# A hybrid encoder layer in fp32: a key product moved to GpSimd, small steps moved to VectorE, ScalarE's order changed in the bidirectional HGRN2 scan

## The reference

```python
f = lb_dir + (1.0 - lb_dir) * jax.nn.sigmoid(f_logits)
kh = 1.0 - f ;  lfh = log(f)
b = jnp.cumsum(log_f, axis=3)                  # in chunks of 32 tokens
scores = (q * exp(b - b_mid)) @ (k * exp(b_mid - b))
contrib = (k * exp(b_last - b)).T @ v ;  decay = exp(b_last)
S_t = decay * S_{t-1} + contrib ;  o = tril(scores) @ v + (q * exp(b)) @ S_{t-1}
o = rmsnorm(o_forward + o_backward, norm_g) * silu(g)
```

## Time and profile before

| what | value |
|---|---|
| median of three runs | 1166.91 us (1166.90 to 1168.83) |
| the profiled execution: own time, span | 1168.83 us, 1166.9 us |
| TensorE busy | 1152.8 us (99%) |
| VectorE, ScalarE, GpSimd busy | 632.5, 457.6, 107.3 us (54%, 39%, 9%) |
| the HGRN2 stage | about 582 to 705 us of the span |

### The profile page before, as it was taken

The page is one execution under the profiler, slowest core; times in us unless marked ns, Lnnn a source line. Parts: engine busy times, 40 slices in busy tenths (PEclk is TensorE's granted clock), DMA queues, the critical chain, the costliest instruction groups (busy, mean ns, idle before and its releaser), DMA issues.

```text
span 1166.9 us, 15661 instructions
## 1 busy us (share of the span) xinstructions
PE 1152.8 (99%) x5879; PEld 935.7 (80%) x5879; DVE 632.5 (54%) x760; ACT 457.6 (39%) x674; POOL 107.3 (9%) x88
## 2 busy tenths in 40 slices
PE   9999999999999999999999999999999999999997
PEld 7888888888888777777778788888888888888886
DVE  6755555543333674444488976656455555552223
ACT  6423322322223444544757745534332232231223
POOL 0000000000001220000057620011000000000000
PEclk9999999999999999999999999999999999999999
DMA  5332233242224232112131122432232322323221
GB/s 202 110 108 101 78 108 107 84 145 97 87 91 168 87 116 72 55 56 71 37 109 38 37 74 91 162 102 97 90 109 90 108 90 90 108 90 108 90 90 72
DMA packets 31677, 111.63 MB, mean 96 GB/s; under 512 B 3984, under 2 KB 5136, under 8 KB 31376
## 3 DMA queue, kind: packets, MB, share of 16 engines
q1 hardware_dynamic: 30192, 104.11, 26.6%
q10 hardware_dynamic: 1440, 6.88, 1.6%
HBM read 105.48 MB, written 4.19 MB: 94 GB/s over the span
## 4 chain that ended last, share of the span: by engine, by line
PE 94%; DVE 2%; ACT 1%; DMA 1%; issue 1%; POOL 0%; ACTq 0%; DVEq 0%; SPq 0%; POOLq 0%
PE ps L1154 25%; PE ps L1156 25%; PE ps L1155 25%; PE ps L1189 3%; PE ps L1188 3%; PE ps L1190 3%; PE ps L1294 1%; PE ps L1303 1%; PE ps L1319 1%; DMA raw<-up_dram 1%; PE ps L1438 1%; PE ps L1421 1%; PE ps L1446 1%; PE ps L1402 0%; DVE w_lo L763 0%
## 5 line engine op out<-in xcount | busy, mean ns | idle before, releaser
L1154 PE MATMUL ps<-h_hi,w_hi 128*128 128x512 f32 x1024 | 408.0, 398 | 0.2 <-DVE w_lo L763 0.2
L1156 PE MATMUL ps<-h_hi,w_lo 128*128 128x512 f32 x1024 | 399.3, 390 | 0.0
L1155 PE MATMUL ps<-h_lo,w_hi 128*128 128x512 f32 x1024 | 399.1, 390 | 0.0
L763 DVE TENSOR_TENSOR w_lo<-raw,w_hi 128x1024 fp32r<-128x1024 f32 (+2 forms) x190 | 233.2, 1230 | 192.5 <-ACT w_hi L419 186.1
L419 ACT ACTIVATE w_hi<-raw 128x1024 fp32r<-128x1024 f32 (+1 forms) x182 | 196.0, 1080 | 172.7 <-PE ps L1156 96.1
L1154 PEld LDWEIGHTS ps<-h_hi,w_hi 128*128 128x128 f32 x1024 | 192.4, 188 | 56.5 <-issue 16.7
L1155 PEld LDWEIGHTS ps<-h_lo,w_hi 128*128 128x128 f32 x1024 | 192.6, 188 | 41.6 <-issue 2.9
L1156 PEld LDWEIGHTS ps<-h_hi,w_lo 128*128 128x128 f32 x1024 | 192.3, 188 | 40.7
L489 ACT ACTIVATE g_hi<-un 128x512 f32 (+1 forms) x44 | 27.8, 632 | 250.8 <-DVE un L763 250.8
L763 DVE TENSOR_TENSOR un<-ps,rs 128x512 f32<-128x512 f32 x44 | 30.4, 691 | 122.2 <-PE ps L1156 122.2
L1154 PE MATMUL ps<-g_hi,w_hi 128*128 128x512 f32 x176 | 68.5, 389 | 0.0
(11 more groups left out here) (238 smaller groups left out, 1239.6 us busy)
## 6 DMA issues: line engine op xcount, KB each, us to landing
raw<-up_dram SPq DMA_DIRECT2D x86, 512.0 KB, 3.2
raw<-proj_dram SPq DMA_DIRECT2D x26, 512.0 KB, 3.3
raw<-down_dram SPq DMA_DIRECT2D x16, 704.0 KB, 4.0
raw<-down_dram SPq DMA_DIRECT2D x22, 512.0 KB, 3.2
raw<-gates_dram SPq DMA_DIRECT2D x16, 512.0 KB, 3.2
raw<-branch_dram SPq DMA_DIRECT2D x8, 512.0 KB, 3.2
raw<-wout_dram SPq DMA_DIRECT2D x8, 512.0 KB, 3.2
x_spill_dram<-xT ACTq DMA_DIRECT2D x1, 2048.0 KB, 7.3
```

The source lines that it names most:

```text
L763: return V.tensor_tensor(out, a, b, op)
L1154: T.matmul(ps[:, bank, :], w_hi[:, slot, cols], moving_hi(j), start=start and j == 0, stop=False)
L1155: T.matmul(ps[:, bank, :], w_hi[:, slot, cols], moving_lo(j), start=False, stop=False)
L1156: ins = T.matmul(ps[:, bank, :], w_lo[:, slot, cols], moving_hi(j), start=False, stop=stop and j == tiles - 1)
```

## The change

- `k_in` is no longer made by ScalarE but by GpSimd, in a new function `key`: a `tensor_scalar` of 128x512 with a scale and a bias for each partition. ScalarE's logarithm, which overwrites its input, waits for it. Keys 0 and 1 are made ahead of GpSimd's loop, key u+2 between `key_to_end` and `values`.
- The 128x16 `fac` difference goes from GpSimd's `to_end` to the end of VectorE's `cumulate`.
- The product with the output gate goes from GpSimd (`gate_outputs`) to VectorE's `normalize`; so does the gain, which had been folded into `silu`. `norm_exp` loses its square, and `normalize` has five operations in place of three.
- Within `exponentials`, `decay` is made ahead of `k_sc` and `k_end`.
- In ScalarE's loop `outputs_to_sbuf` goes behind `exponentials(u + 2)`.
- `WARM` goes from 11 to 8.

```diff
-        FIRST_UNITS, PARTS, PART, WARM, WARM_BANK = 2, 4, UW // 4, 11, 7
+        FIRST_UNITS, PARTS, PART, WARM, WARM_BANK = 2, 4, UW // 4, 8, 7
@@ GpSimd
+            def key(u):
+                pool.wait_ge(fs_done, u + 1)
+                if u == 0:
+                    pool.wait_ge(s_done, 2 * ITEMS)
+                if u >= 2:
+                    pool.wait_ge(ks_done, u - 1)
+                nc.gpsimd.tensor_scalar(k_in[u % 2][:], forget[:, u, :], lb_minus_one[:, u:u + 1], one_minus_lb[:, u:u + 1],
+                                        ALU.mult, ALU.add).then_inc(k_done, 1)
             def to_end(u):
                 pool.wait_ge(b_done, u + 1)
-                if u >= 2:
-                    pool.wait_ge(kfar_done, u - 1)
-                nc.gpsimd.tensor_tensor(fac[:, u % 2, :, :], upper, lower, ALU.subtract).then_inc(fd_done, 1)
-            def gate_outputs(t):
-                nc.gpsimd.tensor_tensor(o_t[:], o_t[:], hgate[:, t, :], ALU.mult).then_inc(og_done, 1)
                 key_to_end(u + 1)
-                if u and u % 2 == 0:
-                    gate_outputs(u // 2 - 1)
+                if u + 2 < TILES:
+                    key(u + 2)
                 if u % 2:
                     values(u // 2 + 1)
@@ ScalarE
             def log_f(u):
-                A(k_in[u % 2][:], forget[:, u, :], ACT.Identity, bias=one_minus_lb[:, u:u + 1],
-                  scale=lb_minus_one[:, u:u + 1]).then_inc(k_done, 1)
+                act.wait_ge(k_done, u + 1)
                 A(forget[:, u, :], forget[:, u, :], ACT.Ln, bias=lb[:, u:u + 1], scale=one_minus_lb[:, u:u + 1]).then_inc(lf_done, 1)
             def exponentials(u):
                 A(fac[:, u % 2, :, :], fac[:, u % 2, :, :], ACT.Exp).then_inc(fac_done, 1)
+                A(decay[u % 2].rearrange("p (e n) -> p e n", n=NSUP)[:, :, n],
+                  ends.unsqueeze(1).to_broadcast([P, HD, NSUP - 1]), ACT.Exp).then_inc(e5_done, 1)
                 A(k_sc[u % 2][:], k_sc[u % 2][:], ACT.Exp, scale=-1.0).then_inc(e2_done, 1)
                 A(k_end[:], k_end[:], ACT.Exp).then_inc(e3_done, 1)
-                A(decay[u % 2].rearrange("p (e n) -> p e n", n=NSUP)[:, :, n],
-                  ends.unsqueeze(1).to_broadcast([P, HD, NSUP - 1]), ACT.Exp).then_inc(e5_done, 1)
             def norm_exp(t):
-                A(o_u[:], o_rs[:], ACT.Square).then_inc(oy_done, 1)
@@ ScalarE's loop
-                if u % 2:
-                    outputs_to_sbuf(u // 2)
                 if u + 2 < TILES:
                     exponentials(u + 2)
                 if u and u % 2 == 0:
                     yb_hi(u // 2 - 1)
+                if u % 2:
+                    outputs_to_sbuf(u // 2)
@@ VectorE, cumulate
+                if u % 2:
+                    tt(fac[:, 1, :, :], b6[:, :, 16:33:16], b6[:, :, 32:49:16], ALU.subtract).then_inc(fd_done, 1)
+                else:
+                    tt(fac[:, 0, :, :], b6[:, :, 31:48:16], b6[:, :, 15:32:16], ALU.subtract).then_inc(fd_done, 1)
             def normalize(t):
-                link(stt(o_u[:], o_u[:], -0.5, o_ms[:], ALU.mult, ALU.mult))
-                link(stt(o_rs[:], o_u[:], 1.5, o_rs[:], ALU.add, ALU.mult))
-                tt(o_u[:], o_t[:], o_rs[:], ALU.mult).then_inc(on_done, 1)
+                link(newton(o_rs[:], o_ms[:], o_u[:]))
+                link(stt(o_t[:], o_t[:], gain[:, 34 + t:35 + t], o_rs[:], ALU.mult, ALU.mult))
+                tt(o_u[:], o_t[:], hgate[:, t, :], ALU.mult).then_inc(on_done, 1)
```

More of the change, by code:

```diff
@@ L318, in _ @@
             supers = lambda t: t.rearrange("p (n c) -> p n c", c=SUPER)
+            def key(u):
[6 more added lines that the diff above has]
+                                        ALU.mult, ALU.add).then_inc(k_done, 1)
             def to_end(u):
                 pool.wait_ge(b_done, u + 1)
-                b3 = supers(b_cum[u % 2][:])
-                if u >= 2:
-                    pool.wait_ge(kfar_done, u - 1)
-                upper, lower = (b3[:, :, 16:33:16], b3[:, :, 32:49:16]) if u % 2 else (b3[:, :, 31:48:16], b3[:, :, 15:32:16])
-                nc.gpsimd.tensor_tensor(fac[:, u % 2, :, :], upper, lower, ALU.subtract).then_inc(fd_done, 1)
                 if u == 0:
@@ L331, in to_end @@
                     pool.wait_ge(kt_done, u)
+                b3 = supers(b_cum[u % 2][:])
                 end = b3[:, :, 0 if u % 2 else SUPER - 1]
@@ L364, in values @@
                                             ALU.mult).then_inc(vexp_done, 1)
-            def gate_outputs(t):
-                pool.wait_ge(osq_done, t + 1)
-                pool.wait_ge(sil_done, HH)
-                nc.gpsimd.tensor_tensor(o_t[:], o_t[:], hgate[:, t, :], ALU.mult).then_inc(og_done, 1)
             pool.wait_ge(spilled, 16)
             nc.gpsimd.memset(q_pad[1], 0.0).then_inc(pad_zeroed, 1)
+            key(0)
+            key(1)
             pool.wait_ge(sil_done, HH)
@@ L389, in _ @@
                     to_end(u + 2)
-            gate_outputs(PAIRS - 1)
             pool.wait_ge(mean_done, 2)
@@ L641, in exponentials @@
                 A(q_sc[:], k_sc[u % 2][:], ACT.Exp).then_inc(e1_done, 1)
+                if u >= 2:
+                    act.wait_ge(state_done, u - 1)
                 act.wait_ge(fd_done, u + 1)
                 A(fac[:, u % 2, :, :], fac[:, u % 2, :, :], ACT.Exp).then_inc(fac_done, 1)
+                n = slice(first, first + NSUP - 1)
+                ends = b[:].rearrange("p (n c) -> p n c", c=SUPER)[:, n, end]
+                A(decay[u % 2].rearrange("p (e n) -> p e n", n=NSUP)[:, :, n],
+                  ends.unsqueeze(1).to_broadcast([P, HD, NSUP - 1]), ACT.Exp).then_inc(e5_done, 1)
                 act.wait_ge(e1_done, u + 1)
@@ L948, in silu @@
                 dve.wait_ge(sl_done, j + 1)
[L949 to L953, removed]
+                dst = (hq, hgate)[j // 4][:, j % 4, :]
+                tt(dst, dst, silu_tmp[j % 4][:], ALU.mult).then_inc(sil_done, 1)
             base = BASE["proj"]
@@ L1016, in cumulate @@
                 tt(chunks(k_sc[u % 2][:]), b3, mid.unsqueeze(2).to_broadcast([P, 2 * NSUP, CHUNK]), ALU.subtract).then_inc(d1_done, 1)
[L1018 to L1024 removed]
+                b6 = supers(b[:])
+                if u % 2:
+                    tt(fac[:, 1, :, :], b6[:, :, 16:33:16], b6[:, :, 32:49:16], ALU.subtract).then_inc(fd_done, 1)
+                else:
+                    tt(fac[:, 0, :, :], b6[:, :, 31:48:16], b6[:, :, 15:32:16], ALU.subtract).then_inc(fd_done, 1)
+            def normalize(t):
+                dve.wait_ge(or_done, t + 1)
+                link(newton(o_rs[:], o_ms[:], o_u[:]))
+                link(stt(o_t[:], o_t[:], gain[:, 34 + t:35 + t], o_rs[:], ALU.mult, ALU.mult))
+                tt(o_u[:], o_t[:], hgate[:, t, :], ALU.mult).then_inc(on_done, 1)
                 dve.wait_ge(on_done, t + 1)
```

10 lines of the change are left out of this document (removed).

## The result

The changed kernel takes **1175.02 us** (median of 4 runs, 1174.26 to 1175.46) against 1166.91, a difference of the medians of +8.1 us. The ratio by all runs is 1.0065, interval 1.0052 to 1.0078. The forecast was 1169.5. The direction was right, the size was off by 5.5 us.

A forecast was written before the change was run, and what follows sets the result against it. TensorE, busy 1152.8 of 1166.9 us, was taken as the bound. 2.2 later at pair 1's `mean_square`, less 1.3, plus a 1.7 clock fall gave +2.6: profiled 1171.4, median 1169.5; own range 1168 to 1171.5, overall 1163.6 to 1172.6.

The forecast's parts named there:

- So 2.0 are left: VectorE's path to the scan of tile 3: 2.0 us of lead left, scan ending at 644.8 in place of 646.8.
- I take nothing: Start: three fewer warm products lengthen TensorE's idle time to about 1.4 us, at no cost; bounds nothing and 1.7.
- Then the same difference holds: Step from profiled time to median: +2.6 applies even if the other runs had no clock fall at A.
- A: TensorE's wait at HGRN2 entry (line 1421, until 601.85): all 1.6 us goes, and the 1.7 clock fall behind it.
- B: TensorE's wait at line 1391 for tile 3, about 1.2 us, ended by ScalarE's mean copy: goes.
- D: TensorE's wait at line 1391 for tile 5 (657.69), 1.28 us, ended by ScalarE's mean copy: goes.
- C: TensorE's wait at line 1438 (646.94), 1.2 us, for VectorE's state scan of tile 3, forecast to end 2.0 earlier.
- The exchange without a fall: Rival 1: waits move as forecast but the clock stays: +0.9, 1167.8 us; chance 0.27.
- The second (all waits go): Rival 2: waits go and none replaces them, scan ending by 641.6; 1160.0 us, halfway 1163.4; chance 0.20.
- The third (keys crowd VectorE): Rival 3: keys 2 to 5 beside VectorE's products delay the scan 3.9 us: 1173.4, at half 1171.5; chance 0.13.
- The fourth, the warm-up: Rival 4: the shorter warm-up costs up to +1.7 us; chance counted within the others.
- D's 1.3 come back: Sum at `mean_square` of pair 1: 2.2 us later, less 1.3 regained from wait D, gives +0.9.

The follow-up runs named there:

- key_decay_order: Kernel before with three queue edits: keys on GpSimd, `decay` ahead, `outputs_to_sbuf` behind the exponentials; `fac`, `normalize`, warm-up as before: 1169.51 us.
- plus_fac: key_decay_order with the `fac` difference also on VectorE: 1171.77 us.
- fac_alone: Changed kernel with one added wait in GpSimd's `to_end`, so `fac` on VectorE never runs beside `k_end`: 1172.83 us.
- plus_norm: key_decay_order with the new `normalize` (gate product, gain and square on VectorE) added: 1171.86 us.
- before_warm8: Kernel before with `WARM` 8 in place of 11, nothing else: 1167.79 us.
- order_only: Kernel before with only ScalarE's order changed, exponentials ahead of `outputs_to_sbuf`: 1170.35 us.
- the best version: keys01_order1: kernel before with keys 0 and 1 on GpSimd and the new ScalarE order in tile 1 alone: 1165.55 us.
- mean_first: Kernel before with ScalarE's copy of the mean put ahead of `log_f`, nothing else: 1167.16 us.
- fac_back: Changed kernel with the `fac` difference on GpSimd again: 1173.88 us.
- norm_back: Changed kernel with the old `normalize`, gate product, gain and square back: 1172.95 us.
- key_decay: Kernel before with keys on GpSimd and `decay` ahead; order, `fac`, `normalize`, warm-up as before: 1172.32 us.
- order_back: Changed kernel with ScalarE's `outputs_to_sbuf` ahead of the exponentials again: 1176.27 us.
- warm11: Changed kernel with eleven warm products again: 1174.35 us.

## Why the size was wrong

**The step that failed is the sum for the scan of tile 3**, "So 2.0 are left", by the prices of `fac` and `normalize`. Without these two edits (and with the gate product left on GpSimd) the same sum gives 2.0 + 0.6 + 1.8 - 1.0 = 3.4 us of lead, an end at 643.4; key_decay_order ended at 641.96 + 1.22 = 643.2. So the rest of the sum held as a total, but by luck in part. The entry was put at 2.2 (bounds 1.4 and 2.6), and key_decay_order has the low part 0.9 earlier (594.70 against 595.58). Against that, tiles 0 and 1, where 0.7 was to be lost on `decay`, lost only 0.1 (the scan of tile 1 at 614.80 against 615.56). The terms of the two edits did not hold:

- *`fac`*: "cost 0.2 each", three on the path, 0.6. Measured 1.02 beside `k_end`, and 2.5 us for the scan (plus_fac). The row was that of an operation alone. The bound of 0.69 was too low as well: I had the row of a VectorE operation stretched from 0.69 to 1.67, and the Trainium skill's rule beside it, and used both for the key and the gate product, not for this one. fac_alone shows the cause.
- *`normalize`*: 1.8 for two more operations, of which the relief of `q_pad` gives back 1.0. Measured 2.2 for the scan (plus_norm; 0.4 of it was there already at `xT`), so about 1.8 in place of 0.8. In the changed kernel pair 0 takes 6.9 us in place of 3.8.
- *The start*: "I take nothing". In before_warm8 the third real unit of products is 0.75 us late (19.12 for 18.37); the changed kernel is 0.75 late at `xT` (576.08), and the median is +0.8 (before_warm8). Where the late start occurred, nothing hid it, but two of the six profiles with eight warm products didn't have it.

Together the changed kernel's scan starts 646.78 - 641.96 = 4.8 us behind that of key_decay_order, 0.75 of it the start, in place of the sum's 1.4. That is 3.4 too little; with the 0.2 by which key_decay_order was early, the scan came 3.2 us later than forecast.

**The second step that failed is the way from the profiled time to the median.** "Then the same difference holds" was wrong. The fall behind A is rare, by all that the runs show: 1.9 us that the median of before never had, and that no change can take from it. It went into the sum unseen, as 1.6 of VectorE's idle 3.42 us; over a kernel before without the fall, key_decay_order has its scan 1.9 us earlier (66.6 against 68.5 behind `xT`) and not 3.6. In profiled executions alone the change costs 1174.64 - 1168.83 = 5.8 against the +2.6 of the sum, 3.2 too little, the same 3.2 as at the scan; the other 1.9 us are this, and 0.4 is the distance of the changed kernel's median from its own profiled time.

**What held.** A shrank and had no fall behind it, and the three other waits went: B and D wholly, C down to 0.8. The entry came only 0.33 us earlier at the low part (595.25 against 595.58), 1.1 without the late start, half of the 2.2 forecast; with the keys alone it came 1.4 earlier (594.16), of which 0.6 was there already at `xT` (574.75), so 0.8. The new wait was 4.34 us for 4.2, its loss of clock 1.71 for 1.7, the wait of pair 0 2.91 for "some 2". A wait of `mean_square` and its place behind the exponentials were the right mechanism, shown by order_only.

**The rivals.** The exchange without a fall is out for the changed kernel. The second (all waits go) needed the scan at 641.6; the best version got it at 643.1. The third (keys crowd VectorE) is out as put: under the new order keys on GpSimd, with `decay` ahead, cost nothing that the runs show. Under the old order it is the key that gets slow beside VectorE, and it holds up ScalarE, +4.0 with the two falls that follow. The fourth, the warm-up, came to 0.8 by the medians.

**"D's 1.3 come back"** fits the changed kernel, where TensorE sets the pace behind the new wait: its `mean_square` of pair 1 starts 5.7 us later than before, and its span is 5.9 longer, where with the 1.7 of lost clock and nothing won back it would be 7.4. By itself it is worth nothing, as mean_first shows. In the kernel before, TensorE and VectorE wait for each other in turn, and what TensorE gains at line 1391 it waits at the scores and at the state.

**What stays open.** Single removals from the changed kernel give 0.7, 1.1 and 2.1 for warm-up, `fac` and `normalize`, additions to key_decay_order 2.2 and 2.3 for the last two. With 5 runs each and ranges of 1.4 to 4.0 us, which is nearer wasn't settled. The profiles say where much of the difference may lie. I take from each profile's own time the clock lost while TensorE worked (changed 1.7, fac_back 1.4, norm_back 2.8, key_decay_order 1.5, plus_fac 3.0, plus_norm 1.7) and its lateness at `xT`. Then, as an estimate from one execution each, `fac` is worth 2.5 taken out and 3.0 put in, `normalize` 1.8 and 2.0. What decides whether a fall is of 1.7 or of 3.4 wasn't found. Why keys with `decay` ahead cost 1.3 more than keys alone was not followed up; the intervals overlap, and the profile of key_decay, with falls of 1.7 and 3.4, is 2.1 above its median.

## What to carry to other kernels

Price an operation by a row in which its neighbour on the other engine runs too: on VectorE a difference of 128x16 elements costs 0.18 us alone and 1.02 beside a GpSimd product, and letting one wait for the other can be the cheaper way. An edit's worth depends on which queue is last: the same keys cost 4.0 us under one order of ScalarE's queue and nothing measurable, with `decay` ahead, under the other, so try queue edits together and per tile, not loop-wide. And look whether the profiled execution is a typical one before you count what can be won in it: a fall of the clock there also lengthens waits of other engines behind it. When you compare two profiles, first take out where each one's stage starts and what its falls cost.

## What the runs showed of the chip

- The clock doesn't fall behind every wait of TensorE. Between 560 and 720 us of the profiles there were falls behind idle times of 1.60 (before), 1.61 (key_decay), 2.35 (order_back), 2.88 us (warm11) and behind all of 3.02 and more; there were none behind 2.91 (changed, plus_fac), 2.90 (norm_back), 2.36 (order_back, at 645.97) and any under 1.60. So between 1.6 and 2.9 us the length alone didn't decide. The two rows of warm11 below are the fall that the changed kernel doesn't have at the same place.
- The clock missing in one such fall, summed over its slices, was 1.7 or 3.4 us. The work behind the wait lost 1.4 to 1.7 or 2.7 to 3.2, less where the clock fell while TensorE still waited.

```profile
629.32 2.07 PE L1373 MATMUL ps<-o_ms,consts 128*128 128x512 f32 x2 [2.88 <-ACT o_ms L679]
...
629.00:630.00 1.00, 0.68 (x1) 0.50 (x2) 0.36 (x1) 1.00 (x2) 0.00 (x0) 0.50 0.00 0
```

- GpSimd's `tensor_scalar` of 128x512 with two scalars for each partition took 0.76 us at its fastest, 0.94 to 1.5 in many tiles, and 2.28 beside VectorE's low part and `q_pad`.
- TensorE's idle time ahead of the first real product was 0.76 us in the profile before and 1.34 with three warm products fewer (before_warm8), and the median was 0.8 us longer (interval -0.5 to 1.6).
